# Loading the gate rows of an attention head once, and moving the gating, the low parts, the last weight turn and the first exponential

## The reference

```python
proj = xn @ w_in
u, zs, cq, ckv, kpe, za = jnp.split(proj, SPLIT_IDX, axis=-1)
q = (rmsnorm(cq, g_qn) @ w_uq).reshape(bsz, seq, N_HEADS, QK_NOPE + QK_ROPE)
q_abs = jnp.einsum('blhd,rhd->blhr', q_nope, w_uk)
c, k_pe = rmsnorm(ckv, g_kvn), rope(kpe, pos)
o = attend(q_abs, q_pe, c, k_pe)                     # causal softmax attention, 8 heads of 128
att_out = o.reshape(bsz, seq, D_ATT) * jax.nn.silu(za)
y = jnp.concatenate([ssm_out, att_out], axis=-1) @ w_out
```

## Time and profile before

| | us |
|---|---|
| median of 3 executions | 1127.38 |
| the three | 1123.99, 1127.38, 1131.94 |
| the profiled execution: its time | 1130.97 |
| its span in the trace | 1128.9 |
| PE busy in the span | 1037.0 (92%) |
| DVE busy | 607.9 (54%) |
| ACT busy | 374.5 (33%) |

### The profile page before, as it was taken

One profiled execution on the slowest core, in us unless ns is written; L12 is line 12 of the kernel. 1 busy time (PEld: TensorE's weight loads), 2 busy tenths in 40 slices (PEclk: granted clock), 3 DMA queues, 4 the chain that ended last, 5 costly groups with the idle time before them and its releaser, 6 DMA issues.

```text
span 1128.9 us, 26833 instructions
## 1 busy us (share of the span) xinstructions
PE 1037.0 (92%) x10642; PEld 958.8 (85%) x10642; DVE 607.9 (54%) x1253; ACT 374.5 (33%) x774; POOL 172.9 (15%) x262
## 2 busy tenths in 40 slices
PE   3899999999999999999699999778888899999995
PEld 2899999999999999989699987555556569999995
DVE  4466354542488842276685536687679642323332
ACT  6322112111232312143651221554446423323333
POOL 2102310000140000010430820313334100000000
PEclk9999999999999999999799999989899999999998
DMA  9445752233343543136535874758789875242213
GB/s 286 105 138 117 153 144 67 77 96 95 95 134 93 140 132 99 61 112 196 158 106 158 236 232 144 248 161 279 235 259 278 273 233 196 75 110 76 74 38 152
DMA packets 201739, 170.93 MB, mean 151 GB/s; under 512 B 37531, under 2 KB 166022, under 8 KB 199814
## 3 DMA queue, kind: packets, MB, share of 16 engines
q1 hardware_dynamic: 178534, 120.16, 37.9%
q0 software_dynamic: 11616, 29.11, 8.7%
q10 hardware_dynamic: 11496, 20.36, 4.9%
HBM read 141.93 MB, written 25.31 MB: 148 GB/s over the span
## 4 chain that ended last, share of the span: by engine, by line
PE 80%; ACT 5%; DMA 5%; DVE 4%; issue 4%; SPq 1%; ACTq 0%; POOL 0%; DVEq 0%; POOLq 0%
PE gemm L2068 13%; PE gemm L2069 12%; PE gemm L2070 12%; PE gemm L2430 6%; PE gemm L2432 5%; PE gemm L2431 5%; PE misc L2339 2%; PE gemm L2353 2%; PE gemm L2381 2%; PE misc L2144 2%; PE misc L2154 1%; DMA w_raw<-w_glu 1%; PE misc L2095 1%; PE gemm L2167 1%; DMA w_raw<-w_in 1%
## 5 line engine op out<-in xcount | busy, mean ns | idle before, releaser
L2068 PE MATMUL gemm<-xh,w_hi 128*128 128x260 f32 (+2 forms) x1056 | 302.3, 286 | 0.6 <-DVE w_lo L1340 0.6
L2069 PE MATMUL gemm<-xl,w_hi 128*128 128x260 f32 (+2 forms) x1056 | 300.7, 285 | 0.0
L2070 PE MATMUL gemm<-xh,w_lo 128*128 128x260 f32 (+2 forms) x1056 | 299.9, 284 | 0.0
L1340 DVE TENSOR_TENSOR w_lo<-w_raw,w_hi 128x2048 fp32r<-128x2048 f32 (+3 forms) x63 | 108.2, 1717 | 226.6 <-ACT w_hi L862 222.8
L862 ACT ACTIVATE w_hi<-w_raw 128x2048 fp32r<-128x2048 f32 (+3 forms) x63 | 90.7, 1439 | 336.2 <-PE gemm L2070 281.4
L2068 PEld LDWEIGHTS gemm<-xh,w_hi 128*128 128x128 f32 x1056 | 198.8, 188 | 1.5 <-DVE w_lo L1340 0.8
L2070 PEld LDWEIGHTS gemm<-xh,w_lo 128*128 128x128 f32 x1056 | 199.1, 189 | 0.0
L2069 PEld LDWEIGHTS gemm<-xl,w_hi 128*128 128x128 f32 x1056 | 198.9, 188 | 0.0
L2430 PE MATMUL gemm<-comb_hi,w_hi 128*128 128x260 f32 x512 | 147.0, 287 | 1.2 <-DVE comb_lo L1948 1.1
L2432 PE MATMUL gemm<-comb_hi,w_lo 128*128 128x260 f32 x512 | 144.8, 283 | 0.0
L2431 PE MATMUL gemm<-comb_lo,w_hi 128*128 128x260 f32 x512 | 144.6, 282 | 0.0
(11 more groups left out here) (383 smaller groups left out, 1976.8 us busy)
## 6 DMA issues: line engine op xcount, KB each, us to landing
w_raw<-w_in SPq DMA_DIRECT2D x35, 1024.0 KB, 6.2
ckv<-cache_ckv POOLq DMA_DIRECT2D x76, 256.0 KB, 3.7
w_raw<-w_out SPq DMA_DIRECT2D x16, 1024.0 KB, 5.8
ckv<-cache_ckv SPq DMA_DIRECT2D x52, 256.0 KB, 3.7
z_d<-ev ACTq DMA_DIRECT2D x16, 260.0 KB, 2.1
w_raw<-w_glu SPq DMA_DIRECT2D x8, 512.0 KB, 4.2
yt<-x_prompt SPq DMA_DIRECT2D x4, 1024.0 KB
o_y_p<-yt SPq DMA_DIRECT2D x4, 1024.0 KB
```

What stands on the lines that cost most here:

```text
L1340: dve.tensor_tensor(w_lo[:, slot, 0:width], w_raw[:, slot, 0:width], w_hi[:, slot, 0:width].bitcast(F32), ALU.subtract).then_inc(w_lo_read ...
L2068: pe.matmul(acc, a, xa, start=k == 0, stop=False)
L2069: pe.matmul(acc, a, xb, start=False, stop=False)
L2070: last = pe.matmul(acc, b, xa, start=False, stop=k == k_tiles - 1)
```

## The change

1. The buffer `za` goes. All eight gate rows are loaded once, straight into `comb[:, 8 + h]`, on SP between the loads of `w_uq` of two kinds of blocks (before `L604`), and `gate_o` multiplies in place. `load_za` and SP's wait for `o_gated` leave the loop.
2. On DVE `gate_o` and `head_lo` move from the steps n % 4 == 0 to n % 4 == 1 (`head_lo(1)` stays in step 1), and on SP `load_raw` and `load_rotary` move from n % 4 == 1 to n % 4 == 2.
3. On PE `turn_last_weights(n - 1)` comes ahead of the fourth page group.
4. On ACT `exponential(0)` comes ahead of the copies to `qa` and of `build_query(0)`.

```diff
-        za = at("za", EV0, [P, 2, NQ])
...
                     load_qn(i * 2 + (2 + u), u)
+            sp.wait_ge(gated, 10)
+            for h in range(N_HEADS):
+                sp.dma_start(comb[:, 8 + h, N_META:T_PROMPT], z_d[D_SSM + h * P:D_SSM + (h + 1) * P, N_META:T_PROMPT]
+                             ).then_inc(ug_loaded[h % 2], 16)
             with sp.Fori(0, 2) as i:
...
-            def load_za(h):
-                sp.dma_start(za[:, h % 2, :], z_d[D_SSM + h * P:D_SSM + (h + 1) * P, N_META:T_PROMPT]).then_inc(ug_loaded[h % 2], 16)
...
-            for h in range(2):
-                load_za(h)
...
-                if n % 4 == 1 and h + 1 < N_HEADS:
+                if n % 4 == 2 and h + 1 < N_HEADS:
                     sp.wait_ge(head_lo_done, h + 1)
                     load_raw(h + 1)
...
                     load_v(h)
-                    sp.wait_ge(o_gated, h - 1)
-                    load_za(h)
...
+            exponential(0)
             act.wait_ge(sample_loaded, 16 * 9)
             act.activation(qa[0:QK_ROPE, 4].rearrange("p b h -> p h b"), qps[0:QK_ROPE], ACT.Copy).then_inc(absorbed_copied, 1)
...
             act.wait_ge(filled, 11)
-            exponential(0)
...
-                tt(comb[:, 8 + h, N_META:T_PROMPT], PVB[:], za[:, h % 2], ALU.mult).then_inc(o_gated, 1)
+                tt(comb[:, 8 + h, N_META:T_PROMPT], PVB[:], comb[:, 8 + h, N_META:T_PROMPT], ALU.mult).then_inc(o_gated, 1)
...
-                if n % 4 == 0 and n:
+                if n % 4 == 1 and n > 1:
                     gate_o(n // 4 - 1)
-                if n % 4 == 0 and n and n // 4 + 1 < N_HEADS:
+                if n % 4 == 1 and n // 4 + 1 < N_HEADS:
                     head_lo(n // 4 + 1)
                 if n == 1:
-                    head_lo(1)
...
                     scores(n + 1)
+                if n % 4 == 0 and n:
+                    turn_last_weights(n - 1)
                 for i in range(N_GROUPS_OF_PAGES - 4):
                     if freed_at(i) == n and i % 4:
                         weigh_pages(i // 4, i % 4)
                 if n % 4 == 0 and n:
-                    turn_last_weights(n - 1)
                     weigh_values(n // 4 - 1)
```

More of the change, by code:

```diff
@@ L1104, in _ @@
             act.activation(cnt[:], latc[:, :, T_PROMPT:T], ACT.Copy).then_inc(absorbed_copied, 1)
-            act.wait_ge(sample_loaded, 16 * 9)
-            act.activation(qa[0:QK_ROPE, 4].rearrange("p b h -> p h b"), qps[0:QK_ROPE], ACT.Copy).then_inc(absorbed_copied, 1)
-            act.wait_ge(absorbed_copied, N_HEADS + 5)
-            act.wait_ge(filled, 10)
-            def build_query(s):
-                if s >= 2:
-                    act.wait_ge(sc_ready, 2 * s - 2)
-                for a in range(4):
-                    rows, cols = slice(32 * a, 32 * a + 32), slice(a * N_HEADS, (a + 1) * N_HEADS)
-                    act.activation(qx[rows, s % 2, :, cols], rep[rows, 0:16, :, s], ACT.Copy)
-                    last = act.activation(qxr[rows, s % 2, :, cols], rep[rows, 16:18, :, s], ACT.Copy)
-                last.then_inc(query_built, 1)
-            build_query(0)
             def exponential(m):
@@ L1136, in exponential, with build_query @@
                                    accum_out=stat[:, SME + at_m:SME + at_m + 1]).then_inc(exp_done, 1)
+            exponential(0)
+            act.wait_ge(sample_loaded, 16 * 9)
+            act.activation(qa[0:QK_ROPE, 4].rearrange("p b h -> p h b"), qps[0:QK_ROPE], ACT.Copy).then_inc(absorbed_copied, 1)
+            act.wait_ge(absorbed_copied, N_HEADS + 5)
+            act.wait_ge(filled, 10)
+            def build_query(s):
+                if s >= 2:
+                    act.wait_ge(sc_ready, 2 * s - 2)
+                for a in range(4):
+                    rows, cols = slice(32 * a, 32 * a + 32), slice(a * N_HEADS, (a + 1) * N_HEADS)
+                    act.activation(qx[rows, s % 2, :, cols], rep[rows, 0:16, :, s], ACT.Copy)
+                    last = act.activation(qxr[rows, s % 2, :, cols], rep[rows, 16:18, :, s], ACT.Copy)
+                last.then_inc(query_built, 1)
+            build_query(0)
             def copy_turned(m):
```

## The result

The changed kernel takes 1140.41 us (median of 5 executions, 1138.45 to 1142.10) against 1128.59 for the kernel before (1123.99 to 1131.94): ratio 1.0094, 95% interval 1.0066 to 1.0123. It is slower by 11.8 us in the medians (their quotient is 1.0105, within the interval); 1136 was forecast, with 1116 to 1148 as the range.

What follows compares the result with a forecast made beforehand. PE was taken as the bound, held in a head's second half by a DVE, ACT, PE loop. Terms -1.5 + 9.0 + 0.3 + 0.6 = +8.4 on 1127.4 gave 1135.8, say 1136 us; range 1116 to 1148.

Steps and rivals of the forecast that it cites:

- The chain: Second half of a head: moved gating and low parts delay DVE's maximum, ACT's exponential, PE's scores; +9.0, and +0.3 at n = 29.
- the exponential, and PE's scores behind it, come 1.5 later: Fourth tile's maximum 1.59 later, cover 0.06 to 0.1; six heads at 1.5 each give +9.0, bounds 0 to 2.6 a head.
- The last weights: PE's turn ahead of the fourth page group: wait ahead of value products stays, both ACT copies 0.1 later, +0.6 in all.
- The bound of -0.7 at n = 4: Only at n = 4, with no output copy ahead, could the wait ahead of the value products shrink, by up to 0.7.
- The first exponential: Ahead of ACT's copies at the loop's start: DVE's awaited page load is issued earlier, -1.5, between -2.9 and -0.9.
- The gate loads: Eight at once on SP near 608: issue hides, the next weight block lands about its split; 0, with +1 as bound.
- Raw rows: Issued one step later on SP: next page load 0.8 later, DVE's need 1.5 later; 0 a head, bound +1.
- D: Rival: page loads behind the raw rows land late, +1 a head on top of the main forecast, 1142; chance 0.11.
- C: Rival: the new wait drops TensorE's clock, 1.3 a head in six heads, +8, time 1144; chance 0.17.
- B: Rival: less traffic and a slacker PE list calm the disturbed heads, up to 17.1 goes, time 1119; chance 0.25.
- The 17.1: Excess of the seven head-loop stretches over 7 x 20.13, taken as waits put down to issue and half clock behind them.
- The rule weighed in the prediction: Instruction fetch is mostly hidden; by it the loop's excess has no such cause and the time stays at 1136.

Runs made afterwards that it cites:

- e1: Changed kernel with gating, low parts and raw rows back in their old steps, the other edits kept: 1130.77 us, ratio 0.9983 to the kernel before.
- e3: Changed kernel with low parts and raw rows back in their old steps, only the gating still moved: 1135.41 us, ratio 1.0003 to the kernel before.
- e7: Like e1, with ACT's copy of the last turned weights ahead of its copy of the sample's output: 1127.70 us, ratio 0.9961.
- e10: Changed kernel with ACT's copy of the last turned weights ahead of its copy of the sample's output: 1135.95 us, ratio 1.0021.
- e11: Changed kernel measured again as it is, on another chip: 1140.51 us, ratio 1.0063 to the kernel before.
- e5: Kernel before with only the gate rows loaded once ahead of `w_uq`, none in the loop: 1129.09 us, ratio 0.9983.
- e9: Kernel before with PE's last-weight turn ahead of the fourth page group and ACT's copy of them ahead of the output copy: 1127.54 us, ratio 0.9943.
- e2: Changed kernel with its eight gate loads issued some 80 us later on SP: 1140.56 us, ratio 1.0066 to the kernel before.
- e4: Changed kernel with 18 added 256-column products on PE in the wait ahead of a head's first scores: 1141.16 us, ratio 1.0077.

## Why the prediction was right

**The chain, and its size.** The step "the exponential, and PE's scores behind it, come 1.5 later" is what happened: 1.52 in an undisturbed head (e1 against the changed kernel), 21.77 where 21.6 was named, and e3 splits it as the working did, by where the 400-column maximum can start. Gating and low parts took 2.53 together, where 2.62 was put. PE's wait was 2.72 for a forecast of 2 to 2.5: the working's own 0.78 + 0.34 + 1.5 is 2.62, and the weight turn comes 0.85 earlier in the head where 0.78 was put. ACT's wait for DVE was 2.43, not 1.5: that counted only the delay, and left out that ACT's own work ahead of it ends some 1.0 earlier.

**The last weights.** "Turning earlier on PE changes nothing there, because ACT copies in the same order" was right: 0.83 against 0.71, +0.12 a head for the +0.1 of the sum, and e7 and e10 show ACT's order as the cause. The profile had put that wait down to issue, though it was one for ACT's copy. The bound of -0.7 at n = 4 was empty: that wait is 0.32 in both profiles.

**The first exponential** was put at -1.5; the page group came 0.7 to 1.9 earlier against ACT's copy, and no ratio shows it. **The gate loads**, put at 0 with +1 as the bound, cost 0.75 at `w_uq`. I had the block land at about the time of its split; its split came 1.2 late. (At 0.48 each, by the row used, the eight issues take 3.8, not 3.6; nothing hung on it.) **Raw rows**: D did not come about. DVE's wait for pages in the loop, 1.6 before, is absent in the changed profile and 0.9 in e11's.

**Where the sum was short.** The chain's +9.3 and the rest of the sum made 8.4, and 7 to 12 were measured. That the spans of the two profiles differ by as much as the sum, 8.6, is partly luck, for the parts don't agree: the loop is 5.2 longer, where +9.9 was put, and the rest 3.4, where -1.5 was put. The kernel before has three of its first six stretches below full clock, e1 only one; against e1, which lacks the move alone, the changed kernel's loop is 8.4 longer (163.17 against 154.76).

In the loop two rivals came in part and against each other. C: four of the first six stretches of the changed kernel show a lower clock. A head with the wait of 2.7 alone takes 21.77 at full clock, 23.32 at a mean clock of 0.93 and 24.44 at 0.86, so 1.6 to 2.7 where it comes, and 1.3 was put. But the ground I gave it was wrong: the same 2.7 is followed by full clock at 880.83 and by half clock at 762.32, and e3 has half clock behind waits of 0.8 and 0.9.

B: waits for issue of 0.5 and over, those ahead of value products left out, sum to 8.5 in the first six stretches before, and to 6.1 to 9.4 in the other kernels without the move (e1, e5 to e9). The kernels with it have 3.1, 5.8 (e11), 4.2 (e2) and 4.5 (e10), but 10.2 where the wait is filled (e4). e5 takes out the traffic alone and keeps 7.05, and e9, which leaves it in, has 8.1, so fewer bytes are not what shrank them. That the time in the new wait is partly time that PE would have waited for instructions fits these sums, and one head of the changed kernel has both, 1.65 for issue at 829.20 and only 0.82 ahead of the scores at 833.38; it is not shown, as e3 has 5.4 with no new wait over 1.11. The 17.1 was also read too widely: in the last head a wait of 2.83 for ACT's scaling stands in every profile, and the prediction counts it to issue and half clock.

The rule weighed in the prediction, that a code block's fetch is mostly hidden (the Trainium skill, "Runtime: NRT & Kernel Launch", Instruction fetch mechanics), holds for 18 of the 23 places counted under e4 and fails at the five that cost 10.2. The one by which transfers of all issuers interleave ("DMA: Bandwidth & Descriptors" of the Trainium skill, Issuing engines are not separate DMA queues) did not make rival B, and the late `w_uq` block says nothing on it, as SP issues both that block and the gate rows ahead of it.

## What to carry to other kernels

Work moved on an engine that is mostly idle is free only if it leaves and enters idle time: look at the wait ahead of its old place and at whose result it now stands in front of. A producer put earlier brings nothing while its consumer's engine keeps another wait ahead of the copy; move both. And filling a wait of the busiest engine need not pay: here the granted clock rose, other waits of the same engine grew, and the time stayed.

## What the runs showed of the hardware

PE's waits for issue of up to 3.5 us inside its page scores are waits for instructions: in thirteen profiles all 64 of 0.45 and over stand behind a multiple of 256 of its matmuls and weight loads, and each ends 1.2 to 1.6 after an instruction packet has come. A change of the list moves them to other instructions. They were shorter or absent in most heads in which PE had stopped for 2.7 before (2.90 in one of e11 all the same); what makes a packet late was not tried.

TensorE's drop to 1.2 GHz is not told by the length of the single wait ahead of it: waits of 2.72 came with and without it, and it came behind two waits of 0.80 and 0.92 that lay 0.7 apart. What decides it stays open.
